# A hybrid decoder layer on one core: input projection by Strassen's seven products in three passes, attention one pass behind

## The reference, cut to what matters

```python
def prompt_layer(x, mem, pre_g, post_g, w_in, conv_w, sinks, mem_g, w_mk, w_mv, w_out):
    h = rms_norm(x, pre_g)
    cb, cc, ch, cz, q, k, v, sz, mq, mz = split(h @ w_in)        # 1024 -> 3072 = 24 tiles of 128
    u = cc * ch                                                  # 384 channels, 3 taps
    y_conv = cb * short_conv(pad(u), conv_w) * silu(cz)
    y_swa = swa_attention(blocks(q), band(k), band(v), sinks) * silu(sz)   # 6 heads, window 128, ALiBi, sinks
    mk, mv = mem_kv(mem, mem_g, w_mk, w_mv)                      # 256 memory tokens, 4 heads
    y_mem = mem_attention(mq, mk, mv) * silu(mz)
    y = concatenate([y_conv, y_swa, y_mem]) @ w_out              # 1024 -> 1024
    return x + rms_norm(y, post_g)                               # and the states of conv, k, v, mk, mv
```

## Time and profile before

| | before |
|---|---|
| median of 3 runs | 855.19 us (854.34 to 855.33) |
| span of the profiled execution, its own time | 853.6 us |
| PE busy | 845.1 us (99%), 5306 matmuls |
| PEld busy | 706.8 us (83%) |
| POOL busy | 600.4 us (70%) |
| DVE busy | 467.1 us (55%) |
| ACT busy | 242.9 us (28%) |
| DMA | 115.9 MB, mean 136 GB/s |
| granted TensorE clock, mean | 0.999 of 2.4 GHz |

### The profile page before, as it was taken

One profiled execution on the slowest core, in us unless ns is written; L12 is line 12 of the kernel. 1 busy time (PEld: TensorE's weight loads), 2 busy tenths in 40 slices (PEclk: granted clock), 3 DMA queues, 4 the chain that ended last, 5 costly groups with the idle time before them and its releaser, 6 DMA issues.

```text
span 853.6 us, 13888 instructions
## 1 busy us (share of the span) xinstructions
PE 845.1 (99%) x5306; PEld 706.8 (83%) x5306; DVE 467.1 (55%) x1020; ACT 242.9 (28%) x669; POOL 600.4 (70%) x802
## 2 busy tenths in 40 slices
PE   9999999999999999999999999999999999999997
PEld 8999999998877877887887778777777887787785
DVE  6428777976352556676543436765445054577414
ACT  6523413312110444232211323431121134224111
POOL 5799575666888666766969675767388985766771
PEclk9999999999999999999999999999999999999999
DMA  9764322127356233216566422222643732222232
GB/s 336 271 223 157 125 74 75 51 63 296 124 173 247 99 99 124 69 56 184 199 194 226 148 99 99 75 74 38 222 130 103 249 106 74 76 74 75 67 155 99
DMA packets 39906, 115.87 MB, mean 136 GB/s; under 512 B 6624, under 2 KB 13024, under 8 KB 39424
## 3 DMA queue, kind: packets, MB, share of 16 engines
q1 hardware_dynamic: 39552, 114.71, 40.2%
q10 hardware_dynamic: 288, 0.27, 0.1%
HBM read 105.73 MB, written 10.26 MB: 136 GB/s over the span
## 4 chain that ended last, share of the span: by engine, by line
PE 92%; POOL 3%; DMA 2%; SPq 1%; DVE 0%; issue 0%; ACT 0%; DVEq 0%; POOLq 0%; ACTq 0%
PE pj L667 68%; PE pa L667 21%; POOL w_lo L619 2%; DMA w_raw<-in_weights 2%; PE pa L819 2%; PE pa L775 1%; POOL w_hi L616 1%; SPq L504 0%; PE pa L693 0%; DVE w_lo L1276 0%; SPq L505 0%; SPq L502 0%; SPq L506 0%; SPq L451 0%; SPq L503 0%
## 5 line engine op out<-in xcount | busy, mean ns | idle before, releaser
L619 POOL TENSOR_TENSOR w_lo<-w_raw,w_hi 128x256 fp32r<-128x256 f32 x516 | 413.5, 832 | 10.8
L667 PE MATMUL pj<-h_hi,w_hi 128*128 128x512 f32 (+2 forms) x936 | 334.1, 357 | 1.8 <-POOL w_lo L619 1.0
L667 PE MATMUL pj<-h_hi,w_lo 128*128 128x512 f32 (+2 forms) x936 | 328.4, 351 | 0.0
L667 PE MATMUL pj<-h_lo,w_hi 128*128 128x512 f32 (+2 forms) x936 | 328.1, 351 | 0.0
L616 POOL TENSOR_SCALAR w_hi<-w_raw 128x512 fp32r<-128x512 f32 x258 | 170.4, 679 | 195.3 <-PE pj L667 155.3
L667 PEld LDWEIGHTS pj<-h_hi,w_hi 128*128 128x128 f32 x936 | 176.4, 188 | 32.2 <-issue 10.1
L667 PEld LDWEIGHTS pj<-h_hi,w_lo 128*128 128x128 f32 x936 | 176.3, 188 | 23.2
L667 PEld LDWEIGHTS pj<-h_lo,w_hi 128*128 128x128 f32 x936 | 176.5, 189 | 21.4
L667 PE MATMUL pa<-w_hi,y_hi 128*128 128x512 f32 x160 | 62.6, 392 | 0.0
L667 PE MATMUL pa<-w_lo,y_hi 128*128 128x512 f32 x160 | 62.4, 390 | 0.0
L667 PE MATMUL pa<-w_hi,y_lo 128*128 128x512 f32 x160 | 62.2, 389 | 0.0
(11 more groups left out here) (212 smaller groups left out, 1012.0 us busy)
## 6 DMA issues: line engine op xcount, KB each, us to landing
w_raw<-in_weights SPq DMA_DIRECT2D x131, 512.0 KB, 3.6
...
```

Source lines behind the costliest of these rows:

```text
L619: last = pool.tensor_tensor(w_lo[slot][:, part], raw[:, part], w_hi[slot][:, part].bitcast(F32), ALU.subtract)
L667: return pe.matmul(out, lhsT, rhs, start=start, stop=stop)
```

## The change

`h @ w_in` is computed by Strassen's method (in Winograd's form) with one level: two weight tiles make a pair, K is cut into two halves of 512, and the tokens of a pass into two halves. For a pair that is a 2 x 2 block product, done by seven products of half-size blocks in place of eight.

- There are three passes of 696, 696 and 688 columns (the first with 664 prompt tokens and the 32 samples), `NW` = 348, 348, 344 being half of each. There are 12 pairs (`PAIRS`), so 36 pairs g in all, each of seven products in the order `ORD`; the first two pairs are interleaved (`START`). A product is 128 outputs x 512 of K x 348 tokens: 12 matmuls of 348 columns (`product`). The step n counts products; every engine's work is placed by n, and there are 260 of them with the memory's eight, then 128 steps of the output projection.
- The seven token operands (sums and differences of quarters) are kept for a pass as seven pairs `h_hi[m]`, `h_lo[m]` of 4 x 348 columns. For the next pass they are staged on DVE (`stage`, 16 multiplications of 348 columns, and four subtractions of 1392) and refilled, one m at a time, as the last pair of the pass lets go of them (`hi_refill` on ACT, `lo_refill` on DVE).
- Four of the seven weight operands are sums. In pass 0 DVE makes them (`w_sum`, 512 columns each, four for each pair), SP stores them in DRAM (`s_d`), and the later passes load them (`load_op`).
- The high parts of the weights are now made by ACT (`hi`, one copy of 512 columns for a product), the low parts by POOL as before (`split`, two TENSOR_TENSOR of 256 columns). The ring has `WS` = 5 slots of one product.
- Products accumulate in PSUM along chains X (1, 6, 7, 4), Y (5, 3) and Z (2). Between them ACT copies the running value out (`copy_of`), and the next product of the chain waits for the copy. Quarters of the result are put together on DVE (`c11`, `c12`, `c21`) and POOL (`c22`).
- Pass 0 still runs on tokens that are not normalised, except that its 1/rms rows now come through DRAM as `r1`; its results are multiplied by it (`times_r`, `c22_r`).
- q, k, v and the gates are stored to DRAM (`store_quarter`) and fetched for each visit (`load_visit`, `load_values`, `load_gates`). Visits 0 to 4 lie in pass 1 (n = 104 to 168), 5 to 10 in pass 2 (n = 190 to 262), 11 to 15 in the output projection. Their parts are the ones of before.
- The output projection comes last, block by block, with all of `w_out` split beforehand into the SBUF that the `h` operands leave (`split_wo`), and `y` through DRAM (`load_y`, `split_y`). It has the same 768 matmuls of 512 columns.

```diff
+NP = 3
+NW = [348, 348, 344]
+PAIRS = [("CC0", "CH0"), ("V0", "K0"), ("Q0", "Q1"), ("Q2", "M0"), ("M1", "Z0"), ("Z1", "Z2"), ("Z3", "Z4"),
+         ("CZ0", "CB0"), ("CC1", "CH1"), ("CZ1", "CB1"), ("CC2", "CH2"), ("CZ2", "CB2")]
+ORD = [1, 5, 6, 2, 7, 3, 4]
+START = [(0, 1), (0, 2), (1, 1), (1, 2), (0, 5), (0, 6), (1, 5), (0, 7), (0, 3), (1, 6), (0, 4), (1, 7), (1, 3), (1, 4)]
+CHAIN = {1: "X", 6: "X", 7: "X", 4: "X", 5: "Y", 3: "Y", 2: "Z"}
...
+PROD = list(START)
+for _g in range(2, NP * NPAIR):
+    if _g == 4:
+        PROD += [("MK", f, h) for f in range(2) for h in range(2)]
+    if _g == 5:
+        PROD += [("MV", x) for x in range(4)]
+    PROD += [(_g, m) for m in ORD]
...
+for _g in range(2, NPAIR):
+    for _i in range(4):
+        S_AT[(base(_g) - 6 + _i) if _g > 2 else 9 + _i] = (_g, _i + 1)
+ATT_S = {0: 104, 1: 117, 2: 130, 3: 143, 4: 156, 5: 190, 6: 202, 7: 214, 8: 226, 9: 238, 10: 250, 11: 268, 12: 286,
+         13: 304, 14: 322, 15: 340}
...
+for _p in range(1, NP):
+    _last = NPAIR * _p - 1
+    for _i in range(18):
+        STAGE_AT[SL[_last, 1] - 20 + _i] = (_p, _i)
+    for _m in ORD:
+        REFILL_HI[SL[_last, _m]] = (_p, _m)
...
+            def load_op(i):
+                g, m = PROD[i]
+                j, pair = RAW_AT[m], g % NPAIR
+                sp.wait_ge(w_split, 2 * (i - RAW + 1))
+                if g == NPAIR:
+                    sp.wait_ge(s_stored, 16 * (NPAIR - 1))
+                if j < 3:
+                    src = w_pairs[pair][:, j * FH:(j + 1) * FH]
+                else:
+                    sp.wait_ge(s_stored, 16 * (pair + 1))
+                    src = s_d[pair][:, (j - 3) * FH:(j - 2) * FH]
...
+            def store_quarter(g, qt):
+                p = g // NPAIR
+                wait_quarter(sp, g, qt)
+                n = NW[p] if qt[1] == "1" else PT[p] - NW[p]
+                a = T0[p] + NW[p] * (qt[1] == "2")
+                sp.dma_start(proj_d[:, KEPT[role(g, qt)], a:a + n], result(g, qt)[:, 0:n]).then_inc(
+                    ev_free[EVI[g, qt] % 3], 16)
...
             def split(n):
-                slot, raw = n % WS, w_raw[n % RAW]
-                pool.wait_ge(w_loaded[n % RAW], (n // RAW + 1) * 16)
-                if n >= WS:
-
-                    pool.wait_ge(proj_done, last_unit(SEQ[n - WS]))
+
+                for i, part in enumerate(halves):
+                    if i == 0 or n == 0:
+                        pool.wait_ge(w_his, n + 2 if n else 1 + i)
+                    if i == 0 and n >= WS:
+                        pool.wait_ge(prod_done, n - WS + 1)
+                    pool.tensor_tensor(w_lo[n % WS][:, part], raw_of(n)[:, part], w_hi[n % WS][:, part].bitcast(F32),
+                                       ALU.subtract).then_inc(w_split, 1)
...
+            def c22(g):
+
+                pool.wait_ge(copied, COPIED[g, 7])
+                wait_result(pool, g, "22")
+                out, w = result(g, "22"), NW[g // NPAIR]
+                ins = pool.tensor_tensor(out, u3[:, 0:w], m5[g % 2][:, 0:w], ALU.add)
+                if g < NPAIR and stored(role(g, "22")):
+                    return step(ins)
+                ins.then_inc(c22_done, 1)
+
+            def c22_r(g, token):
+                need(token)
+                pool.wait_ge(r1_loaded, 2 * 16)
+                out = result(g, "22")
+                pool.tensor_tensor(out, out, r1[:, cols_of(g, "22")], ALU.mult).then_inc(c22_done, 1)
...
+            def product(n):
+                g, m = PROD[n]
+                p = g // NPAIR
+                w, c = NW[p], CHAIN[m]
+                wh, wl = parts_of_w(n, 4)
+                out = banks[BANK[g, c]][:, 0:w]
+                opens = m in (1, 5, 2)
+                if opens:
+                    wait_chain(pe, BEFORE[g, c])
+                else:
+                    pe.wait_ge(copied, COPIED[g, {6: 1, 7: 6, 4: 7, 3: 5}[m]])
+                new = FIRST_USE[p, m] == n
+                if new and p:
+                    pe.wait_ge(h_ready[m], 4 + p)
+                for k in range(4):
+                    if k % 2 == 0:
+                        pe.wait_ge(w_split, 2 * n + 1 + k // 2)
+                    if new and p == 0:
+                        pe.wait_ge(h_ready[m], k + 1)
+                    cols = slice(k * w, (k + 1) * w)
+                    last = terms(out, wh[:, k, :], wl[:, k, :], h_hi[m][:, cols], h_lo[m][:, cols], opens and k == 0,
+                                 k == 3, True)
+                last.then_inc(prod_done, 1)
+
...
+            def copy_of(n):
+
+                g, m = PROD[n]
+                if m not in (1, 5, 6, 7):
+                    return
+                act.wait_ge(prod_done, n + 1)
+                if m == 1 and g:
+                    act.wait_ge(c11_done, g)
+                if m == 6 and g:
+                    act.wait_ge(c12_done, g)
+                if m == 7 and g:
+                    act.wait_ge(c22_done, g)
+                if m == 5 and g > 1:
+                    act.wait_ge(c22_done, g - 1)
+                out, w = {1: m1, 6: u2, 7: u3, 5: m5[g % 2]}[m], NW[g // NPAIR]
+                copy(out[:, 0:w], banks[BANK[g, CHAIN[m]]][:, 0:w], scale_of(names_of(g)[m in (7, 5)])).then_inc(copied, 1)
+
...
+                    copy(w_hi[n % WS][:, part], raw[:, part]).then_inc(w_his, 1)
...
+            def hi_refill(p, m):
+                w = NW[p]
+                act.wait_ge(prod_done, SL[NPAIR * p - 1, m] + 1)
+                if m in SCALED:
+                    act.wait_ge(scaled_x, 16 * (p - 1) + SCALED[m])
+                else:
+                    act.wait_ge(staged, 4 * (p - 1) + STAGED[m])
+                copy(h_hi[m][:, 0:4 * w], staged_in[m][:, 0:4 * w]).then_inc(h_his, 1)
...
+            def lo_refill(p, m):
+                w = NW[p]
+                dve.wait_ge(h_his, hi_count(p, m))
+                sub(h_lo[m][:, 0:4 * w], staged_in[m][:, 0:4 * w], h_hi[m][:, 0:4 * w]).then_inc(h_ready[m], 1)
+                if m in (1, 5):
+                    dve.wait_ge(h_ready[m], 4 + p)
+                if m == 1:
+                    dve.tensor_tensor(quad[0][:, 0:4 * w], quad[3][:, 0:4 * w], temp[:, 0:4 * w], ALU.subtract).then_inc(
+                        staged, 1)
+                if m == 5:
+                    dve.wait_ge(staged, 4 * (p - 1) + STAGED[6])
+                    dve.tensor_tensor(temp[:, 0:4 * w], quad[1][:, 0:4 * w], quad[0][:, 0:4 * w], ALU.subtract).then_inc(
+                        staged, 1)
...
+            def w_sum(g, s):
...
+                    ins = dve.tensor_tensor(a[:, 4, :], a[:, 3, :], a[:, 2, :], ALU.add)
+                elif s == 2:
+                    if g < 2:
+                        dve.wait_ge(first_a[g][0], 16)
+                    dve.wait_ge(s_made, S_MADE[g, 1])
+                    ins = dve.tensor_tensor(a[:, 5, :], a[:, 4, :], a[:, 0, :], ALU.subtract)
+                elif s == 3:
+                    ins = dve.tensor_tensor(a[:, 3, :], a[:, 0, :], a[:, 3, :], ALU.subtract)
+                else:
+                    if g < 2:
+                        dve.wait_ge(first_a[g][1], 16)
+                    dve.wait_ge(s_made, S_MADE[g, 2])
+                    ins = dve.tensor_tensor(a[:, 6, :], a[:, 1, :], a[:, 5, :], ALU.subtract)
+                ins.then_inc(s_made, 1)
...
+            def c11(g):
+
+                w = NW[g // NPAIR]
+                dve.wait_ge(prod_done, SL[g, 2] + 1)
+                dve.wait_ge(copied, COPIED[g, 1])
+                wait_result(dve, g, "11")
+                add_scaled(result(g, "11"), banks[BANK[g, "Z"]][:, 0:w], scale_of(names_of(g)[0]), m1[:, 0:w]).then_inc(
+                    c11_done, 1)
...
+            def times_r(g, qt):
+
+                dve.wait_ge(r1_loaded, 2 * 16)
+                dve.wait_ge(c11_done if qt == "11" else c12_done, g + 1)
+                out = result(g, qt)
+                dve.tensor_tensor(out, out, r1[:, cols_of(g, qt)], ALU.mult).then_inc(scaled_r, 1)
...
+            def load_visit(v):
+                gr, mp = v // 2, v % 2
+                if v == 0:
+                    sp.wait_ge(w_split, 2 * NPAIR * 7 + 16)
+                    sp.wait_ge(s_stored, 16 * NPAIR)
+                    sp.wait_ge(sy_ready, 2)
+                else:
+                    sp.wait_ge(sw_s, NH * v)
+                    sp.wait_ge(mm_s, v)
+                wait_stored(sp, max(pass_of(v * P + P - 1), pass_of(gr * 2 * P + 2 * P - 1)))
+                sp.dma_start(q_in[:], proj_d[:, KEPT["Q0"]:KEPT["Q0"] + G, v * P:(v + 1) * P]).then_inc(att_loaded, 16)
+                a = P if v == 0 else 0
+                sp.dma_start(k_in[:, a:], proj_d[:, KEPT["K0"], v * P - P + a:(v + 1) * P]).then_inc(att_loaded, 16)
+                sp.dma_start(mq_in[:], proj_d[:, KEPT["M0"] + mp, gr * 2 * P:(gr + 1) * 2 * P]).then_inc(att_loaded, 16)
...
```

2645 lines of the change are left out of this document (1420 added, 1225 removed).

## The result

The changed kernel takes **993.6 us** (median of four, 992.5 to 995.2) against 854.9 of the kernel before on the same chip: a ratio of 1.162 (95% interval 1.161 to 1.164), slower by 16%. The forecast was 849.5 with a range of 808 to 885. Its span is 991.1 us.

The account below looks back on a forecast made before the run. PE's matmuls, one start after the other, were taken to bound the kernel. From the 853.6 us span, -62.7 + 12 + 33 + 6 + 6 gave 847.9, plus 1.6 to the median 849.5 us; range 808 to 885.

Parts of the forecast that it names:

- Step 1: Products of the input projection: 3024 matmuls, 0.157 us for 348 columns, 62.7 us saved.
- Step 2: Start: PE waits for token operands that DVE makes and leaves at 49 us instead of 32.6, +12 us.
- Step 3: Rest of pass 0: POOL, pushed back by DVE, paces PE with 190 us against 150, +33 us.
- step 5: Visits: half a us for each of 11 among the products, +6 us; DRAM loads and stores at no cost.
- rival B: Pass 0: DVE's instructions also wait for POOL and DVE becomes the bound, +61 instead of +33: 877 us; chance 0.24.
- Step 4: Later passes: PE bounds again; only the refill of pass 2 costs, +6 us (0 to 15).
- Rival D: Late DRAM transfers hold each of 16 visits by 1 us, a few more at sums: 868 us; chance 0.07.
- Rival A: Pass 0: DVE's and POOL's instructions fall between each other and cost nothing: 816 us, or 812; chance 0.22.
- C: Pass 0: a PE with gaps loses the granted clock, 50 us of work at 1.2 GHz: 875 us; chance 0.05.

Follow-up runs that it names:

- e4: Changed kernel with POOL's low parts of the weights made for only 16 of every 256 columns from the sixth product on: 909.0 us, 1.064.
- e15: Changed kernel with 1/rms written to DRAM as rows, nine places for results and POOL's low parts on 16 of 256 columns: 881.2 us.
- e1: Changed kernel with 1/rms written to DRAM as rows instead of 4-byte elements: 974.3 us, 1.139.

## Why the prediction was wrong, step by step

*Step 1 was right*: 0.158 us a matmul against 0.157, and 63 us saved.

*Step 2, the start, was too small*: 58.5 us, not 49. DVE was as full as I said (9.8, 9.4 and 8.7 us busy of each ten from 10 to 40 us), and its last low part was made at 43.1 us, before my 47. But I let PE leave as soon as the last operand was there. It stopped before the eighth product from 29.8 to 42.3 us, and then had seven products to do: 7 x 1.9 = 13.2, and 3 more at half clock.

*Step 3 had the right size for the turns, by luck, and the wrong mechanism.* POOL's subtractions cost 30.5 us in pass 0 against my 33. But pass 0 ended at 307.4 us, not 232: the rest of it took 248.9 where I had 183, and most of the difference is step 5's. I said that POOL would pace PE. POOL was busy 164.3 of 248.9 us, its `w_lo` waited for ACT, and PE never waited for POOL in that stretch. It is DVE that is made late: 148.9 us busy against 108.3 with rows and thin low parts, 0.22 us for each of the 183 instructions of rival B, which I had at over 0.4.

*Step 4 is the step that failed*, with "PE bounds again". I compared the sum of an engine's work (129 us of POOL) with PE's, found room, and put 6 us to the refill. Pass 1 took 225.0 us and pass 2 236.9, where the forecast had 188 and 199, its visits included: 75 us. POOL's subtractions, and the turns that they bring, are 48 of them by `e4`. A visit is a chain, scores, maximum, exponential, scaling, transposes, on engines that work in order, and each of DVE's links with two inputs in SBUF was 0.25 to 0.34 us longer on average beside a POOL that reads SBUF. Spare time of DVE on average (150 of 225 us busy) covers none of that. With the turns away, pass 1 is 199.4 and pass 2 214.6 (`e15`), still 27 us above the forecast. There PE waits 21 us in the two passes, for DVE's `mo_sum` (7.6), `prob` (5.7), results and gates (4.5) and for copies (3.6), and loses 4 at half clock; what makes DVE late there was not tried.

*Step 5 failed too, with "no cost is put to them".* I weighed the way through DRAM by its bytes over the whole span. What was measured of it lies in pass 0 and comes by landing: 19.4 us for the elements of 1/rms, 8 for stores that hold three places, and the two stops of 7 and 9 us in `e15`. The first of these waits for 1/rms to come back, issued behind a 1 MB store; the second for a block of rows while the DMA engines are 0.99 busy. In passes 1 and 2 of the changed kernel DVE waited 17.6 and 14.3 us for landings too, and no run took these away. Rival D had the mechanism, but in the visits and at 1 us each.

*Rivals.* A's cover didn't hold (and half of 6 + 6 off its 816 is 810, not 812). C, the clock, I took as a case apart; it follows every stop, 27.2 us in the changed kernel, 16.2 with thin low parts, 13.0 in `e15`. B had the right engine and the wrong bound: DVE was made late, but it was busy for 148.9 of 248.9 us, nowhere near full.

In one line, from the changed kernel to `e15`: 993.6 - 19.4 (elements) - 84.6 (POOL's subtractions and their turns, with the half clock that goes with them) - 7.2 (ring) = 882.4 against 881.2 measured. Rival A, the forecast without turns, was 816. The 65 us between are by stretch: start 54.8 against 49, rest of pass 0 186.3 against 150, pass 1 199.4 against 188, pass 2 214.6 against 199, and the output 5 shorter than forecast. Of pass 0's 36, its stops are 27.8 and the half clock 4.6.

What stays open: the late sample visits (5.0 and 6.8 us at 214 and 240 us in `e1`; about gone with thin low parts) were not tried by themselves; nor was a start in which DVE has less to do, a `w_mem` that is waited for piece by piece, or a larger ring in the later passes.
